# Layer 0's opening in two halves of the features, and a weight group of the attention stage taken two steps earlier

## What is computed

```python
def modulate(cvec, w_mod_l, b_mod_l):
    m = jnp.einsum('bd,de->be', jax.nn.silu(cvec), w_mod_l) + b_mod_l
    return jnp.split(m[:, None, :], N_MOD, axis=-1)     # sh1, sc1, g1, sh2, sc2, g2
...
h = rmsnorm(x, norm1_l) * (1 + sc1) + sh1
p = jnp.einsum('btd,de->bte', h, w_in_l)                # mixer projections
```

## Time and profile before

| | before |
|---|---|
| median of three executions | 1338.06 us |
| the profiled execution | 1338.34 us |
| its span | 1336.3 us |
| PE busy | 1279.6 us, 96% of the span |
| DVE busy | 613.7 us, 46% |
| ACT busy | 358.8 us, 27% |
| POOL busy | 152.5 us, 11% |
| DMA over the span | 234 GB/s on average |

### The profile page before, as it was taken

One profiled execution on the slowest core, in us unless ns is written; L12 is line 12 of the kernel. 1 busy time (PEld: TensorE's weight loads), 2 busy tenths in 40 slices (PEclk: granted clock), 3 DMA queues, 4 the chain that ended last, 5 costly groups with the idle time before them and its releaser, 6 DMA issues. The chain is left out here.

```text
span 1336.3 us, 17216 instructions
## 1 busy us (share of the span) xinstructions
PE 1279.6 (96%) x6042; PEld 735.3 (55%) x6042; DVE 613.7 (46%) x1519; ACT 358.8 (27%) x931; POOL 152.5 (11%) x257
## 2 busy tenths in 40 slices
PE   6999999999999999999999999989999999999997
PEld 3555555565666564444455555566666656444443
DVE  0132266444566463433343224655556536344438
ACT  1121255434343210000012114563444311100001
POOL 2210220000000110000142003000000011000014
PEclk9999999998999999999999999999899999999999
DMA  9976996499111489999694038430201139999966
GB/s 355 363 248 220 347 332 254 162 359 327 42 64 64 168 333 398 361 374 367 260 334 161 16 140 291 151 128 15 88 33 64 63 130 352 404 368 360 362 270 246
DMA packets 125441, 313.16 MB, mean 234 GB/s; under 512 B 9882, under 2 KB 58426, under 8 KB 112688
## 3 DMA queue, kind: packets, MB, share of 16 engines
q1 hardware_dynamic: 90896, 243.13, 49.8%
q0 software_dynamic: 12848, 45.39, 9.0%
q10 hardware_dynamic: 21616, 23.60, 5.3%
HBM read 232.14 MB, written 80.71 MB: 234 GB/s over the span
## 5 line engine op out<-in xcount | busy, mean ns | idle before, releaser
L790 PE MATMUL ps<-ring,big 128*128 128x384 f32 (+2 forms) x640 | 230.7, 520 | 1.7 <-DVE big L1773 1.3
L790 PEld LDWEIGHTS ps<-ring,big 128*128 128x128 f32 x640 | 120.3, 190 | 104.6 <-issue 63.7
L871 PE MATMUL ps<-ring,arena 128*128 128x512 f32 x384 | 169.3, 594 | 1.9 <-ACT arena L1406 1.9
L502 PEld LDWEIGHTS ps<-consts,arena 128*128 128x128 f32 (+2 forms) x880 | 103.7, 143 | 79.1 <-issue 50.9
L502 PE MATMUL ps<-consts,arena 128*128 128x128 f32 (+2 forms) x880 | 129.7, 278 | 15.7 <-ACT arena L1227 6.6
L711 PE MATMUL ps<-ring,big 128*128 128x512 f32 x320 | 143.0, 598 | 0.8
L563 PE MATMUL ps<-arena 64*128 64x128 f32 (+5 forms) x576 | 137.9, 430 | 6.1 <-DVEq L1822 3.4
L1227 ACT ACTIVATE arena<-ps 128x384 f32<-128x384 f32 (+3 forms) x140 | 69.1, 493 | 221.3 <-PE ps L502 221.3
L871 PEld LDWEIGHTS ps<-ring,arena 128*128 128x128 f32 x384 | 71.2, 190 | 83.1 <-issue 83.1
L563 PEld LDWEIGHTS ps<-arena 64*128 64x128 f32 (+1 forms) x576 | 79.4, 196 | 65.8 <-issue 57.8
L711 PEld LDWEIGHTS ps<-ring,big 128*128 128x128 f32 x320 | 59.0, 190 | 70.4 <-issue 66.4
(11 more groups left out here) (237 smaller groups left out, 1481.9 us busy)
## 6 DMA issues: line engine op xcount, KB each, us to landing
ring<-in_w_mod SPq DMA_DIRECT2D x40, 1024.0 KB, 11.8
ring<-in_w_up SPq DMA_DIRECT2D x22, 1024.0 KB, 9.7
ring<-in_w_gate SPq DMA_DIRECT2D x22, 1024.0 KB, 7.6
slots<-zeros ACTq DMA_DIRECT2D x8, 2560.0 KB, 14.4
slots<-zeros SPq DMA_DIRECT2D x8, 2560.0 KB, 20.2
arena<-in_w_down SPq DMA_DIRECT2D x16, 1024.0 KB, 12.7
arena<-slots SPq DMA_DIRECT2D x30, 512.0 KB, 6.4
slots<-arena POOLq DMA_DIRECT2D x30, 512.0 KB, 9.6
```

The costliest lines, as they stand in the source:

```text
L502: return pe.transpose(out, in_, ident)
L790: mm = pe.matmul(ps[:, c, 0:CHUNKS[c][1]], hT[:, s, k, :], slot[c][:, k, 0:CHUNKS[c][1]], start=(k == 0), stop=(k == KD - 1))
L871: mm = pe.matmul(ps[:, b, :], xgT[:, b, k * P:(k + 1) * P], w_gu[q][:, :, k, :], start=(k == 0), stop=(k == KD - 1))
```

## The change

The opening of layer 0 is done in two halves of the features, a = 0 (features 0 to 511) and a = 1 (512 to 1023). For each half SP loads the columns of `w_mod` that modulate these features (a chunk of the shift and a chunk of the scale, 4 MB, in two parts) and the rows of `w_in` that multiply them (all four chunks, k 4a to 4a + 3). PE modulates the first half, turns it into columns, runs the first tile's four chunks over k 0 to 3, and leaves the sums open in PSUM; then it does the same for the second half. ACT's part of the first tile (features 0 to 511) needs only half 0, DVE's part only half 1. Even and odd k are summed in separate strips, and a DVE reduction adds them.

In phase 2 group 1 runs at steps 1 and 3 in place of 3 and 4; the spins of steps 1 and 3 are gone, and the column turning behind it comes one step earlier (5 in place of 6). Groups 2 and 0 of the next layer stay at their steps. ACT runs one small exponential before phase 2.

```diff
-MOD_AT = (3, 10, 17)
+MOD_AT = ((1, 3), (10, 11), (17, 18))
...
+            def first_mods(a, ks):
...
+                pe.wait_ge(mod0_in[2 * a + ks[0] // 4], 32)
+                for k in ks:
+                    for v in range(2):
+                        i = 2 * v + k % 2
+                        mm = pe.matmul(ps[32 * i:32 * i + 32, 7, :], sc[:, k, :], slot0[2 * v + a][:, k, :],
+                                       start=(k < 2), stop=(k >= KD - 2), tile_position=(0, 32 * i))
...
+            def first_tile():
+
+                pe.wait_ge(h_half, 1)
+                for half in range(2):
+                    S[half].take(pe, ("in", 0, 0))
+                for a in range(2):
+                    if a == 1:
+                        spin(6, 4)
+                        first_mods(1, range(0, 4))
+                        spin(6, 4)
+                        first_mods(1, range(4, KD))
+                        first_columns(1)
+                        pe.wait_ge(T.free, T.freed[("h", 0, 0)])
+                    for half in range(2):
+                        pe.wait_ge(slot_in[2 * a + half], 32)
+                        for c in (2 * half, 2 * half + 1):
+                            for k in range(4 * a, 4 * a + 4):
+                                mm = pe.matmul(ps[:, c, 0:CHUNKS[c][1]], hT[:, 0, k, :], slot[c][:, k, 0:CHUNKS[c][1]],
+                                               start=(k == 0), stop=(k == KD - 1), skip_group_check=True)
...
-                        if s == 3:
-                            spin(7, 3)
...
-                        if s < 2:
+                        if s == 0:
                             spin(7, 4)
...
-                            if s in (at, at + 1) and (g < 2 or L < DEPTH - 1):
-                                ks = range(4 * (s - at), 4 * (s - at) + 4)
+                            if s in at and (g < 2 or L < DEPTH - 1):
+                                ks = range(4 * at.index(s), 4 * at.index(s) + 4)
...
-            for quarter in range(4):
-                mod_group(0, 0, range(2 * quarter, 2 * quarter + 2))
-                if quarter == 2:
-                    pe.wait_ge(head_in, 16)
-                    turn_entry(0, 0)
-                if quarter < 3:
-                    spin(3, 6)
-            mod_columns(0)
-            spin(3, 5)
+            first_mods(0, range(0, 4))
+            spin(3, 8)
+            pe.wait_ge(head_in, 16)
+            turn_entry(0, 0)
+            first_mods(0, range(4, KD))
+            first_columns(0)
+            spin(3, 3)
...
+            for a in range(2):
+                for part in range(2):
+                    ks = slice(4 * part, 4 * part + 4)
+                    for i in (a, 2 + a):
+                        sp.dma_start(slot0[i][:, ks, :], w_mod[:, ks, i * 512:(i + 1) * 512]).then_inc(mod0_in[2 * a + part], 16)
+                    if (a, part) == (0, 0):
+                        x_load(t_in["x0"], 0)
+                        sp.dma_start(consts[:, 0:HEAD], t_in["consts"][:, 0:HEAD]).then_inc(head_in, 16)
+                ks = slice(4 * a, 4 * a + 4)
+                for c in range(4):
+                    at, w = CHUNKS[c]
+                    sp.dma_start(slot[c][:, ks, 0:w], w_in0[:, ks, at:at + w]).then_inc(slot_in[2 * a + c // 2], 16)
+                if a == 0:
+                    x_load(t_in["x0"], 1)
...
+                act.activation(stat["es"][:, 0:1], mhalf[:, 0:1], ACT.Exp)
                 attention(L, 2)
...
+            pool.memset(y2[:, :, 0:512], 0.0).then_inc(zero_set, 1)
...
-                    pool.wait_ge(M.full, M[("mc", 0)])
+                    pool.wait_ge(M.full, M[("mc", 0, 1)])
                     vector_loads(0)
```

More of the change, by code:

```diff
@@ L95, in ring_loads @@
     for L in range(DEPTH):
-        out += [("in", L), ("out", L)]
+        out += [("in", L), ("out", L)] if L else [("out", L)]
     return out
@@ L102, in slot_no @@
     loads = [k for k in ring_loads() if i >= 2 or k[0] != "out"]
-    return 16 * (loads.index(key) + 1)
+    return 32 + 16 * (loads.index(key) + 1)
 def soon_no(L, i):
@@ L1305, in h_evict @@
                 act.wait_ge(T.full, T[("h", L, i)])
-                act.wait_ge(mc_done, L + 1)
+                if (L, i) == (0, 0):
+                    act.wait_ge(cols_half, 1)
+                else:
+                    act.wait_ge(mc_done, L + 1)
                 if i:
@@ L1508, in vector_loads @@
                 pool.dma_start(sink[:, :], t_in["swa_sink"][L:L + 1, :].broadcast_to([P, 4])).then_inc(vec_in, 16)
-            for g in range(3):
+            bm = t_in["b_mod"][0].rearrange("(g i n) -> i g n", g=3, i=4)
+            for i in range(4):
+                pool.dma_start(y2[32 * i:32 * i + 2, i % 2:i % 2 + 1, 0:512],
+                               bm[i:i + 1, 0:1].broadcast_to([2, 1, 512])).then_inc(bmod_in, 16)
+            for g in (1, 2):
                 bias_loads(0, g)
@@ L1667, in mod_rows, with first_rows_of, first_columns_of @@
                 dve.sem_inc(M.free, 1)
+            def first_rows_of(a):
+                dve.wait_ge(M.full, M[("mod", 0, 0, a)])
+                if a == 0:
+                    dve.wait_ge(bmod_in, 192)
+                TT(y2[:, a, 0:512], ps[:, 7, :], y2[:, a, 0:512], ALU.add).then_inc((rows_half, mods_done)[a], 1)
+                dve.wait_ge((rows_half, mods_done)[a], 1)
+                dve.sem_inc(M.free, 1)
+            def first_columns_of(a):
+                dve.wait_ge(M.full, M[("mc", 0, a)])
+                dve.wait_ge(head_in, 16)
+                columns = ps[:, 7, :].rearrange("p (c v q r) -> p r v c q", c=4, v=2, q=2)
+                for r in range(2):
+                    last = dve.tensor_reduce(modc[:, r, :, 4 * a:4 * a + 4], columns[:, r], AX.X, ALU.add)
+                then(dve, "dve", last)
+                dve.sem_inc(M.free, 1)
+                scale = modc[:, :, 1, 4 * a:4 * a + 4]
+                STT(scale, scale, 1.0, n1c[:, 0:1, 4 * a:4 * a + 4].broadcast_to([P, 2, 4]), ALU.add,
+                    ALU.mult).then_inc((cols_half, mc_done)[a], 1)
             def mod_columns(L):
@@ L2024, in _ @@
                 if L == 0:
-                    mod_rows(0, 0)
-                    mod_columns(0)
+                    for a in range(2):
+                        first_rows_of(a)
+                        first_columns_of(a)
+                        if a == 0:
+                            h_scale(0, 1)
                 h_evict(L, 0)
```

75 lines of the change are left out of this document (40 added, 35 removed).

## The result

Six executions of the changed kernel took 1344.1 to 1350.05 us, median 1347.77; six of the kernel before 1335.75 to 1342.05, median 1338.44. The ratio is 1.0067 with a 95% interval of 1.0048 to 1.0086: slower by 0.7%, 9.3 us between the medians. The profiled execution is one of the quicker ones, 1345.15 us with a span of 1343.0, so 6.7 us of the 9.3 can be looked for in its trace.

A forecast was written before the change was run, and what follows sets the result against it. PE's own order was taken to bound the kernel from 9.29 us on. Opening +1.8, phase 2 of layer 0 +2.6, layer 1 -1.4 gave +3.0; lost clock 2.6 made +5.6: 1343.7 us, range 1340.0 to 1347.0.

The forecast's parts named there:

- the term for DVE behind step 5: Phase 2, layer 0: step 4 no longer lets DVE catch up 3.6 us, costing 0.1 us more (0 to +0.6).
- The opening, +1.8: Opening of layer 0: a second chain costs more than the waiting and spins removed; first tile ends near 59.3, +1.8 us.
- the chain of 3.8 us: Opening: bias, turning, columns and modulating the tile between modulation and projection; the second one takes 3.8 us (3.2 to 4.2).
- The stall, 4.6 us: Phase 2, layer 0, step 1: PE asks for weights at 165.05, they land at 169.7, a new wait of 4.6 us.
- Step 5 at 184.5: Phase 2, layer 0: with stall and moved half groups, step 5 starts at 184.5 instead of 182.0, +2.5 us.
- a forecast of -1.4: Phase 2, layer 1: stall of only 0.6 us, step 5 earlier; -1.4 us with DVE's 0.1 (bounds -2.0 and -0.8).
- I take it that it falls: Phase 2, layer 0: the 4.6 us stall, with the spins of steps 1 and 3 gone, drops the granted clock to half.
- I take 2.6 us: Phase 2, layer 0: price of the clock's fall, 2.6 us, between nothing and 3.6 us for a half group at half speed.
- The sum for phase 2 of layer 0: Phase 2, layer 0: +2.6 us at full clock, from +2.5 and DVE's 0.1, and 2.6 us for the lost clock.
- I expect no slack downstream: Whole kernel after 9.29 us: every microsecond by which a PE step ends later ends the kernel later; later loads move with PE.
- Rival 2: Opening: the clock falls in the second chain too, costing 3.4 us; 1347.1 or 1344.5 us in all; chance 0.15.
- rival 1: Phase 2, layer 0: the clock holds despite the stall, +3.0 us in all, 1341.1 us (1340.0 to 1342.6); chance 0.27.

The follow-up runs named there:

- repeat 1: The changed kernel run again unaltered, on one chip with the kernel before: median 1346.45 us, ratio 1.0063; its profiled execution took 1348.57 us.

## Why the prediction was wrong

The way was right, slower, and the places were right. The size was not: +5.6 forecast, +9.3 measured, 0.8 us beyond the upper end of the range. **The step that failed most is the term for DVE behind step 5, "0.1 more, bounds 0 and +0.6"**: it was 1.2 in layer 0, and in layer 1 it left 0.2 of a gain of 1.4. After it come the clock, 3.4 in place of 2.6, and one profile taken for all executions.

With phase 4 taken alike the first profile stands 8.8 us behind, 3.2 more than forecast: opening -0.5, stall and steps +0.2, clock +0.8, DVE +1.1 in layer 0, layer 1 +1.2, and 0.4 behind layer 1's phase 2, which the opening alone shows too and whose cause is open.

- **The opening, +1.8 (bounds 1.1 to 2.5): held.** +1.3 in the profile, with the weights in time, the chain of 3.8 us (the half group ends at 40.93 + 1.92 = 42.85, the next projection starts at 46.52: 3.7) and no new wait. The last weights are later than the sum had them, near 38.6 and not 37.5 (read in the kernel without spins ahead of them), but PE asks at 40.93.
- **The stall, 4.6 us: held,** 4.75 measured, and 4.74 without the new opening. The zero writes moved away took it to nothing. "Step 5 at 184.5", +2.5, held as well: 2.7 without the clock's share.
- **"Step 4 gave DVE 3.6 us to catch up before, which it now lacks: 0.1 more": failed.** After step 5 the distance grows from 7.5 to 8.6: PE waits 0.68 us for DVE at step 6 and more behind. In layer 1 the same term takes back the gain: -1.3 at step 5, -0.2 at phase 3, for a forecast of -1.4. (The opening alone, with phase 2 as before, shows 0.1 and 0.3 of this.) The order of work on DVE was costed by one step only; the bias addition of 0.68 us and the normalising that DVE had done by then now stand ahead of step 5's maxima. That this order is the cause is read from the rows; no kernel moved the bias addition alone.
- **"I take it that it falls": held. "I take 2.6 us" was short.** The forecast had one fall and at most 3.6 us. In two of the three profiles of the change there are two of 3.4 us, one behind the stall and one behind step 3, which lost its spins; each makes a half group 5.34 in place of 3.64 us, 3.4 together, and nothing behind them hid it. In the third there is one of 6.8 us, from 169.8 while PE still waits: 5.82 and 3.64, 2.2 us. With the first fall taken away by spins 1.8 us came back.
- **The sum for phase 2 of layer 0** was 2.6 + 2.6 = 5.2; the three profiles of the change show 7.3, 7.3 and 6.1 (the differences from the end of the first tile to phase 3).
- **"I expect no slack downstream", one execution for all: failed as a way to the median, though it cost little here.** The low stretches at the start of both layers' phase 4, which are in the kernel before too, last 6.8 us in one execution and 13.6 or 17 in another. Three profiles of the same code end 6.1, 10.1 and 8.5 us behind the one of before. That the first ends within 0.5 us of the +5.6 is luck: a shorter stretch gave 2.7 back.
- Rival 2, a fall in the opening, was set beside the forecast with 0.15 as a case of its own. It comes in some executions on top of the rest, at 1.7 to 2.8 us for a price of 3.4. Its time, 1347.1, is close to the measured one by luck: the first profile and repeat 1 reach theirs without such a fall.
- The bounds of rival 1, 1340.0 to 1342.6, and with them the low end of the range, were counted from the profiled execution's 1338.34; from the median of 1338.06, as the rest, they are 1339.8 to 1342.4. It changes nothing in the outcome.

What stays open: why the change draws more long stretches than before. The mean clock of its executions is 0.986 or 0.987 in seven of twelve and 0.991 in the rest; of the 64 executions of before in the experiments 52 have 0.991 to 0.994. Two falls of 3.4 us in phase 2 account for 0.0025 of this, the step from 0.993 to 0.991. Whether the rest is chance was not settled by three profiles. It is also open why the clock falls where it does; no run here separates what PE does before a fall from the moment at which it comes.

## What to carry to other kernels

A wait on loads is found by comparing, for every load that the moved work needs, its landing with the new time of asking, not with the old one: here a row of the trace (issue 157.06, 12.6 us to landing) told the stall to 0.15 us. Spins on zeros that look like waste may keep a clock (here ten of them kept a half group at 3.64 us), and a group of work taken out of a step takes the catching up of the other engines with it: follow their queues for several steps, not one. And where the clock can fall, one profile is one draw: look at the granted clock of several executions before a difference of a few microseconds is put down to code, and compare profiles with their low stretches taken alike.

## What the runs showed that I had not expected

The clock fell at places where PE had hardly any idle time (6.57 of 6.80 us busy before the stretch of the earlier trace rows), and differently from one execution to the next: in the change's opening not at all or for 3.4 us, and for 6.8 in two kernels with the same opening; at the start of layer 1's phase 4, whose code all these kernels share, for 6.8, 10.2, 13.7 or 17 us. Executions of the changed kernel differ by 5 us with it (1344.0 to 1349.3 in the repeat), in groups by their mean clock (0.991 and 0.986). The kernel before does it too: beside the repeat it took 1335.1 to 1348.1 us, two of seventeen executions at 1348 with 0.983 and 0.985. That is more than most of the parts studied here are worth.

The Trainium skill, "TensorE: Matmul & The Clock Gate", section "Part 1: The HAM clock gate", which the prediction weighed, says that the default state is throttled and activity releases it. The trace agrees for the stall: a wait of 4.75 to 4.82 us ended in the low clock in all three profiles of the change. It doesn't tell all falls: PE's longest idle piece in the 6.8 us ahead of the second fall was 1.56 us, and ahead of the one at 298 in the kernel before under 0.3 us.
